# Two decoder layers with a grouped-expert stage: the down product by split parts too

## The reference, cut to what matters

```
hid = silu(einsum('bsd,edf->bsef', h, w_gate)) * einsum('bsd,edf->bsef', h, w_up)
moe = einsum('bsef,bse,efd->bsd', hid, combine, w_down)
```

## Time and profile before

| | us |
|---|---|
| median of 3 runs | 2462.12 (2461.95 to 2464.5) |
| the profiled execution | 2463.01 |
| its span, first to last instruction | 2461.3 |
| PE busy | 2312.6 (94%) |
| DVE busy | 1416.3 (58%) |
| ACT busy | 1004.6 (41%) |
| POOL busy | 495.6 (20%) |

### The profile page before, as it was taken

The page is one execution under the profiler, slowest core; times in us unless marked ns, Lnnn a source line. Parts: engine busy times, 40 slices in busy tenths (PEclk is TensorE's granted clock), DMA queues, the critical chain, the costliest instruction groups (busy, mean ns, idle before and its releaser), DMA issues.

```text
span 2461.3 us, 33198 instructions
## 1 busy us (share of the span) xinstructions
PE 2312.6 (94%) x12222; PEld 1761.7 (72%) x12222; DVE 1416.3 (58%) x2621; ACT 1004.6 (41%) x1865; POOL 495.6 (20%) x457
## 2 busy tenths in 40 slices
PE   5999999988899999999989999999798999999997
PEld 4897787886575466777668978778766744677775
DVE  6637765554644634666486376654555455356664
ACT  2523333534443123666424233344444422246662
POOL 1002235011000210444200023330200022014440
PEclk9999999999999999999999999999898999999999
DMA  8322232231216653766272222321221284526652
GB/s 254 101 80 73 81 100 80 71 108 56 73 56 219 214 195 123 278 236 239 100 250 88 82 77 87 121 73 59 75 78 56 77 287 161 222 94 252 242 193 109
DMA packets 202110, 333.73 MB, mean 136 GB/s; under 512 B 31200, under 2 KB 162144, under 8 KB 185696
## 3 DMA queue, kind: packets, MB, share of 16 engines
q1 hardware_dynamic: 179024, 305.32, 36.5%
q0 software_dynamic: 19296, 19.98, 2.6%
q10 hardware_dynamic: 3632, 6.31, 0.7%
HBM read 352.48 MB, written 51.38 MB: 164 GB/s over the span
## 4 chain that ended last, share of the span: by engine, by line
PE 82%; DVE 7%; ACT 3%; issue 2%; SPq 2%; DMA 2%; POOL 1%; POOLq 0%; DVEq 0%; ACTq 0%
PE ps L733 77%; PE ps L731 6%; DVE ring_rounded L1799 1%; SPq L569 1%; DVE ssq L1911 1%; DMA ring<-in_ada_w 1%; DVE nmax L1936 1%; SPq L592 1%; DVE spare L1781 0%; DVE H L1894 0%; DVE H_rounded L1904 0%; DVE ps L1933 0%; DMA ring<-in_w_in 0%; ACT WH_rounded L1364 0%; DVE SQKV L1913 0%
## 5 line engine op out<-in xcount | busy, mean ns | idle before, releaser
L733 PE MATMUL ps<-H_rounded,WH_rounded 128*128 128x512 f32 x768 | 308.4, 402 | 0.0
L733 PE MATMUL ps<-X_rounded,WH_rounded 128*128 128x512 f32 x640 | 287.2, 449 | 9.9 <-DVE ring_rounded L1799 3.6
L1799 DVE TENSOR_TENSOR ring_rounded<-ring,WH_rounded 128x512 fp32r<-128x512 f32 (+2 forms) x168 | 198.2, 1188 | 152.9 <-ACT WH_rounded L1364 152.1
L733 PE MATMUL ps<-WH_rounded,X_rounded 128*128 128x256 f32 (+1 forms) x960 | 273.0, 284 | 6.9 <-issue 6.9
L733 PE MATMUL ps<-ring_rounded,X_rounded 128*128 128x256 f32 (+1 forms) x960 | 271.2, 282 | 0.0
L733 PE MATMUL ps<-WH_rounded,H_rounded 128*128 128x256 f32 (+1 forms) x960 | 271.1, 282 | 0.0
L733 PE MATMUL ps<-X_rounded,ring_rounded 128*128 128x512 f32 x640 | 253.5, 396 | 0.0
L1364 ACT ACTIVATE WH_rounded<-ring 128x512 fp32r<-128x512 f32 (+2 forms) x168 | 163.6, 983 | 184.9 <-PE ps L733 66.9
L733 PE MATMUL ps<-Y,ring 128*128 128x512 f32 x512 | 221.2, 593 | 1.9 <-ACT Y L1462 1.9
L733 PE MATMUL ps<-lmask,ident 128*128 128x256 f32 x784 | 190.8, 400 | 5.1 <-issue 3.1
L733 PEld LDWEIGHTS ps<-WH_rounded,X_rounded 128*128 128x128 f32 x960 | 184.1, 192 | 9.7 <-issue 9.6
(11 more groups left out here) (365 smaller groups left out, 4552.6 us busy)
## 6 DMA issues: line engine op xcount, KB each, us to landing
ring<-in_w_in SPq DMA_DIRECT2D x272, 256.0 KB, 3.9
ring<-in_ada_w SPq DMA_DIRECT2D x128, 256.0 KB, 4.9
Y<-in_moe_w_down SPq DMA_DIRECT2D x18, 1024.0 KB
ring<-in_w_branch SPq DMA_DIRECT2D x64, 256.0 KB, 5.2
ring<-in_moe_w_down SPq DMA_DIRECT2D x14, 1024.0 KB, 7.1
gate_logits<-CM SPq DMA_DIRECT2D x44, 256.0 KB, 2.6
TM<-in_moe_w_gate SPq DMA_DIRECT2D x10, 1024.0 KB, 4.9
TM<-in_moe_w_up SPq DMA_DIRECT2D x10, 1024.0 KB
```

The lines of the kernel that those rows point to most:

```text
L733: ins = nc.tensor.matmul(o, lhsT, rhs, start=start, stop=stop)
L1799: ins = v.tensor_tensor(low[j][:, at:at + size], ring[:, j, at:at + size], high[i][:, at:at + size].bitcast(F32), ALU.subtract)
```

## The change

The down product is made of split parts as gate_up is. ScalarE rounds the down weights of block j-1 in two pieces (`down_high`) at the head of iteration j into one single buffer (`down_hi`, in a free part of SQKV), VectorE writes the low parts over the weights (`down_low`). The hidden rows get a high part (ScalarE) and a low part (VectorE), both read from PSUM. Both halves of the result rows are copied by ScalarE. The last of the four pieces of the gate and up weights is moved behind the turned rows, on ScalarE and VectorE, for every block.

```diff
+        down_lo = [rounded(n, i * SLOT, SLOT) for n, i in (("Y", 2), ("Y", 3), ("ring", 2), ("ring", 3))]
+        down_hi = rounded("SQKV", D, SLOT)
...
-        hidden_T = heads(sc[:, 4 * S:4 * S + FF], 2)
+        hidden_ps = heads(ps[:, 3, 0:FF], 2)
+        hidden_hi, hidden_lo = (heads(rounded("SC", 4 * S + i * FF, FF), 2) for i in range(2))
...
                     eng.wait_ge(hidden_ready[i], p.so_far(hidden_ready[i]))
-                    if j:
-                        eng.wait_ge(hidden_copied, p.so_far(hidden_copied))
                     for k in range(2):
                         ins = turn(ps[:, 3, tt(k)], hidden[i][:, k::2], last=k == 1)
                     ins.then_inc(hidden_turned, p.gives(hidden_turned))
-                    p.mark(hidden_copied)
 
                 def down(j):
 
-                    s = (3 * j + 2) % SLOTS
-                    w = heads(experts[s], 2)
-                    eng.wait_ge(hidden_copied, p.so_far(hidden_copied))
-                    if SEQ[j] < NE:
-                        eng.wait_ge(expert_loaded[s], p.next(expert_loaded[s], 16))
+                    wh, wl = heads(down_hi, 2), heads(down_lo[j % AHEAD], 2)
+                    eng.wait_ge(act_ready, p.next(act_ready, 3))
                     for f in range(2):
                         if j:
                             eng.wait_ge(y_ready[f], p.so_far(y_ready[f]))
                         for k in range(2):
-                            ins = mm(bank((6, 1)[f]), hidden_T[:, k], w[:, k, f * 512:(f + 1) * 512], k == 0, k == 1,
-                                     last=k == 1)
+                            at = slice(f * 512, (f + 1) * 512)
+                            ins = three(bank((6, 1)[f]), (hidden_hi[:, k], hidden_lo[:, k]), (wh[:, k, at], wl[:, k, at]),
+                                        k == 0, k == 1)
                         ins.then_inc(down_done[f], p.gives(down_done[f]))
...
(ScalarE)
-                    for q in range(4):
+                    pair_pieces(j, range(3))
+
+                def pair_pieces(j, qs):
+
+                    for q in qs:
                         act(piece(pair_hi[j % 2], q), piece(pair_w[j % AHEAD], q), ACT.Copy).then_inc(
                             act_high, p.gives(act_high))
 
+                def down_high(j):
+
+                    at = (3 * j + 2) % SLOTS
+                    if SEQ[j] < NE:
+                        eng.wait_ge(expert_loaded[at], p.next(expert_loaded[at], 16))
+                    for q in range(2):
+                        half_w = slice(q * D, (q + 1) * D)
+                        act(down_hi[:, half_w], down_w[j % AHEAD][:, half_w], ACT.Copy).then_inc(
+                            act_high, p.gives(act_high))
+
                 pair_high(0)
                 turn_copy(0)
+                pair_pieces(0, (3,))
                 for j in range(BLOCKS + 1):
                     i = j % 2
+                    if j:
+                        down_high(j - 1)
                     if j + 1 < BLOCKS:
                         pair_high(j + 1)
...
                     if j + 1 < BLOCKS:
                         turn_copy(j + 1)
+                        pair_pieces(j + 1, (3,))
                     if j:
                         k = (j - 1) % 2
-                        eng.wait_ge(down_done[0], p.next(down_done[0]))
-                        if j >= 3:
-                            eng.wait_ge(y_stored[k], p.next(y_stored[k], 16))
-                        act(y_rows[k][:, 0:512], bank(6), ACT.Copy).then_inc(y_ready[0], p.gives(y_ready[0]))
+                        for f in range(2):
+                            eng.wait_ge(down_done[f], p.next(down_done[f]))
+                            if f == 0 and j >= 3:
+                                eng.wait_ge(y_stored[k], p.next(y_stored[k], 16))
+                            act(y_rows[k][:, f * 512:(f + 1) * 512], bank((6, 1)[f]), ACT.Copy).then_inc(
+                                y_ready[f], p.gives(y_ready[f]))
                     if j < BLOCKS:
                         eng.wait_ge(hidden_turned, p.next(hidden_turned))
-                        act(hidden_T, bank3(3, 2, P), ACT.Copy).then_inc(hidden_copied, p.gives(hidden_copied))
+                        act(hidden_hi, hidden_ps, ACT.Copy).then_inc(act_high, p.gives(act_high))
...
(VectorE; pair_low takes the pieces as an argument)
+                def down_low(j):
+
+                    for q in range(2):
+                        half_w = slice(q * D, (q + 1) * D)
+                        eng.wait_ge(act_high, p.next(act_high))
+                        v.tensor_tensor(down_lo[j % AHEAD][:, half_w], down_w[j % AHEAD][:, half_w],
+                                        down_hi[:, half_w].bitcast(F32), ALU.subtract).then_inc(
+                            act_ready, p.gives(act_ready))
+
-                pair_low(0)
+                pair_low(0, range(3))
                 turn_low(0)
+                pair_low(0, (3,))
                 for j in range(BLOCKS + 1):
                     i = j % 2
+                    if j:
+                        down_low(j - 1)
                     if j + 1 < BLOCKS:
-                        pair_low(j + 1)
+                        pair_low(j + 1, range(3))
                     if j < BLOCKS:
                         eng.wait_ge(silu_ready, p.next(silu_ready))
                         v.tensor_tensor(hidden[i], gated[i], ps[:, 4 + i, FF:2 * FF], ALU.mult).then_inc(
                             hidden_ready[i], p.gives(hidden_ready[i]))
                     if j + 1 < BLOCKS:
                         turn_low(j + 1)
-                    if j:
-                        k = (j - 1) % 2
-                        eng.wait_ge(down_done[1], p.next(down_done[1]))
-                        if j >= 3:
-                            eng.wait_ge(y_stored[k], p.next(y_stored[k], 16))
-                        v.tensor_copy(y_rows[k][:, 512:1024], bank(1)).then_inc(y_ready[1], p.gives(y_ready[1]))
+                        pair_low(j + 1, (3,))
+                    if j < BLOCKS:
+                        eng.wait_ge(act_high, p.next(act_high))
+                        v.tensor_tensor(hidden_lo, hidden_ps, hidden_hi.bitcast(F32), ALU.subtract).then_inc(
+                            act_ready, p.gives(act_ready))
```

More of the change, by code:

```diff
@@ L2427, in turn_low, with pair_low @@
                             act_ready, p.gives(act_ready))
-                def pair_low(j):
-                    for q in range(4):
+                def pair_low(j, qs):
+                    for q in qs:
                         eng.wait_ge(act_high, p.next(act_high))
@@ L2448, in _ @@
                         turn_low(j + 1)
-                    if j:
-                        k = (j - 1) % 2
-                        eng.wait_ge(down_done[1], p.next(down_done[1]))
-                        if j >= 3:
-                            eng.wait_ge(y_stored[k], p.next(y_stored[k], 16))
-                        v.tensor_copy(y_rows[k][:, 512:1024], bank(1)).then_inc(y_ready[1], p.gives(y_ready[1]))
-                for k in range(2):
-                    p.mark(y_stored[k], 16)
+                        pair_low(j + 1, (3,))
[3 more added lines that the diff above has]
+                            act_ready, p.gives(act_ready))
                 for t in range(NT):
```

## The result

| | before | after |
|---|---|---|
| median of 5 runs, us | 2462.12 (2458.56 to 2464.91) | 2474.66 (2472.57 to 2477.59) |
| profiled execution (span), us | 2463.01 (2461.3) | 2474.19 (2472.5) |
| PE busy | 2312.6 (94%) | 2304.1 (93%) |
| DVE busy | 1416.3 (58%) | 1506.4 (61%) |
| ACT busy | 1004.6 (41%) | 1109.0 (45%) |

The ratio is 1.0046, 95% interval 1.0033 to 1.006: slower by 8 to 15 us. The forecast was 2475.0 (2464 to 2482). TensorE is busy for 8.5 us less than before, and the kernel is slower.

The account below looks back on a forecast made before the run. PE alone bounded the kernel before; after, a two-block loop across engines would. Start and middle 2.6, tail falls 2.2, start clock fall 1.6 us, times two layers, gave 12.9 us more: 2475.0 us median, range 2464 to 2482.

Parts of the forecast that it names:

- two-block loop: Stage middle: a chain from block j's release through TensorE, ScalarE and VectorE to block j+2's; 19.89 us per two blocks.
- one-block loop: Stage middle: a chain through the turn copies and the weight piece put behind the turned rows; 9.575 us a block.
- block 1 later: Stage start: block 1's gate/up released 2.70 us later, with no down product there to cover the delay.
- block 2 later, at full clock: Stage start: block 2's gate/up release 2.2 us later than before, leaving out any clock fall.
- clock fall in block 1's product: Stage start: half clock after a 2.4 us TensorE gap costs 1.6 us a layer, bounds 0 and 3.4.
- the middle: 20 blocks after the third, each 0.09 us shorter: 1.8 us a layer gained.
- tail at full clock: Stage end: the last block's down weights are rounded later, so the end comes 2.2 us later a layer.
- tail's clock fall: Stage end: after 4.1 us of TensorE stillness the last down product runs at half speed; 2.2 us, bounds 0 and 2.7.
- rival C: Stage middle: handover waits lengthen the two-block loop to 20.3 us, 8 us more in all, 2483 us; chance 0.13.
- A: Stage start: the clock holds there and falls only in the tail; 2471.8 us; chance 0.27.
- B: Stage middle: PE stays the bound, the faster side; 2447 us; chance 0.15, including a loop halfway to it.
- D: Every block: weights arrive late, so the split product has no effect; 2480 us or more; chance 0.05.

Follow-up runs that it names:

- e1: Changed kernel with the down product's low x high matmuls left out (8 instead of 12 a block); 2460.11 us, ratio to before 0.9985.
- e4: Changed kernel with two buffers for the rounded down weights, their rounding moved ahead of the row copies; 2454.28 us, ratio to before 0.9966.
- e6: Changed kernel with VectorE again copying the second half of the result rows; 2468.52 us, ratio to before 1.0033.
- e2: Changed kernel with all four gate and up weight pieces again ahead of the silu; 2470.49 us, ratio to before 1.0027.
- e3: Changed kernel with matmuls on constants filling TensorE's stillness before block 1's gate/up and the last down product; 2471.33 us, ratio to before 1.0035.
- e5: Changed kernel with the edits of e4 and e2 together: two buffers, all four pieces ahead; 2435.74 us, ratio to before 0.989.
- e7: The e5 kernel with VectorE copying the second half of the result rows; 2497.28 us, ratio to before 1.0136.

## Why the prediction was right

Step by step, for one layer; shifts are counted from block 0's turns.

| step of the prediction | forecast | measured |
|---|---|---|
| 12 rounded matmuls in place of 3.44 us | 2.72 | 2.78 |
| two-block loop | 19.89 | 19.77 (9 turns from 1013.86 to 1191.93: 19.79) |
| one-block loop | 9.575 | 9.59 (e1), 9.57 (e4) |
| block 0 later | +1.35 | +1.37 |
| block 1 later | +2.70 | +2.74 |
| block 2 later, at full clock | +2.2 | +2.3 |
| clock fall in block 1's product | +1.6 | +1.53 (7.32 - 5.79) |
| the middle | -1.8 | -2.8 |
| tail at full clock | +2.2 | +2.2 |
| tail's clock fall | +2.2 | +1.54 (4.60 - 3.06) |
| sum of the last five rows | +6.4 | +4.8 |

The mechanism was right in each step, and the experiments bear on all but one of them singly: e1 and e6 shorten the two-block loop by a known amount, e4 breaks it, e2 takes the late start away, e3 the clock falls, e5 everything at once. The tail's longer wait has no experiment to itself; it goes with the loop in e4 and e5, where PE stands still for 1.19 us ahead of the last down product instead of 4.07. Two terms were mis-sized. The loop is 0.12 us shorter than worked out: the row copy starts 9.47 us after the release (1013.86 to 1023.33) where I had 9.56, because the down product starts 6.42 us after it (1020.28) where I took 6.54 from the one such block of before (its matmuls then take 0.02 longer than worked out); the rest is in VectorE's five pieces (5.68 for 5.71). Over ten turns that is the 1.0 us by which the middle differs. And the tail's product was slowed for part of its length only: the clock was 0.52 from 1214.40 to 1217.00 and 0.85 over the 3 us after. The 2.2 us I had taken is about what the same stillness cost in e2. Together 1.6 us a layer, 3.2 in all. That the median fell within 0.4 us of the forecast is luck: the two stages grew by 9.5 us where 12.9 were forecast, unchanged stretches of the profiled execution were 1.7 us longer, and the two medians lie by 1.4 us further apart than the two profiled executions, at 12.5, with an interval of 8 to 15. The sum is also 0.1 out by its own rounding (2 x 6.4 is 12.8), and the range ends at 2482 where rival C stands at 2483.

Of the rivals, A (the clock holds at the start) did not happen in either layer: 7.32 and 7.29 us for block 1's product. B (PE stays the bound) is what e5 shows, but it needed another order and a second buffer. C's longer loop fell by 19.77. D's late weights did not occur in the changed kernel; they did in e7, from a queue the prediction had only noted as unchanged.

The rule named from the Trainium skill, page "TensorE: Matmul & The Clock Gate", section "Part 1: The HAM clock gate", that idling brings the lower clock, agrees with both falls: 0.51 after 2.38 us and 0.52 after 4.07 us of stillness. The other, page "ScalarE: Activation LUTs", section "What ACT_TABLE_LOAD costs", would have made the loop 0.03 longer than my rows; the step of the row copy is 0.49 us in the trace after too (1023.33 to 1023.82), and the loop measured was shorter than both.

## What to carry to other kernels

Engine sums of 8.2, 8.7 and 9.3 us a block say nothing about the period until the loops through in-order queues are added up: write one instruction chain from a product back to itself, count how many blocks it spans, and divide. When a faster product hands its saving to such a loop, look for the instruction that forces the order (here the reuse of one buffer, which puts the next rounding behind this product's result copy) and give it a second place, before shaving durations. Price the first and last block by themselves: a piece that is hidden in the middle stands bare there, and look at how long TensorE stands still there: 2.38 and 4.07 us of stillness were each followed by half clock and cost 1.5 us (4.07 us cost 2.3 in e2), while 2.07 us ahead of block 0 cost nothing.

## What the runs showed of the hardware that I had not expected

GpSimd's issue of a row store, 1.0 us in most blocks, took 4.86 to 4.91 us in seven blocks of e7 and not in e5 (1.04 at most); before, the longest was 1.83. All seven start while VectorE works on its four pair pieces. And the fall of the clock costs much the same each time in block 1: 1.5 us in layer one (7.32) and in layer two (7.29), in e1 (7.37), e4 (7.36) and e6 (7.33). In the tail it does not: 4.60 us in layer one of the changed kernel, 5.32 in e2.
